# A two-layer hybrid trunk on 8 cores: interleaved spatial-gating stage, prefetches in flight together, the first eight weight blocks cast on chip, and weight copies stored in other passes

## What is computed

```
h = x
xn = rmsnorm(h);  p = xn @ ab_w_in                      # layer 0: pooling mixer A and short convolution B
h = h + concat(a_out, b_out) @ ab_w_out
h = h + square(relu(rmsnorm(h) @ mlp_w1[0])) @ mlp_w2[0]
xn = rmsnorm(h);  p = xn @ cd_w_in                      # layer 1
u, v = split(gelu(p[..., :1024]))
s = einsum('gts,bnsgc->bntgc', tril(w_s), layernorm(v)) + b_s     # 128-position chunks
c_out = u * s
d_out = stick_breaking_attention(q, k, v)               # 8 heads of 64, strictly causal
h = h + concat(c_out, d_out) @ cd_w_out
h = h + square(relu(rmsnorm(h) @ mlp_w1[1])) @ mlp_w2[1]
return rmsnorm(h)
```

## Time and profile before

| | us |
|---|---|
| median of 3 runs | 2937.12 (2935.02 to 2939.16) |
| the profiled execution's own time | 2936.28 |
| its span on the slowest core, first to last instruction | 2934.7 |
| spans of the 8 cores | 2916.7 to 2934.7 |
| PE busy (matmuls) | 2804.6, 96% of the span |
| DVE, ACT, POOL busy | 1462.7, 1415.3, 1184.9 |

### The profile page before, as it was taken

One profiled execution on the slowest core, in us unless ns is written; L12 is line 12 of the kernel. 1 busy time (PEld: TensorE's weight loads), 2 busy tenths in 40 slices (PEclk: granted clock), 3 DMA queues, 4 the chain that ended last, 5 costly groups with the idle time before them and its releaser, 6 DMA issues.

```text
span 2934.7 us, 43323 instructions; the slowest of 8 cores (2916.7 to 2934.7 us)
## 1 busy us (share of the span) xinstructions
PE 2804.6 (96%) x13273; PEld 1198.4 (41%) x13273; DVE 1462.7 (50%) x1759; ACT 1415.3 (48%) x2407; POOL 1184.9 (40%) x1685
## 2 busy tenths in 40 slices
PE   8899989999999999899999999999999989999998
PEld 3344433444444343344444344444444434444443
DVE  3501245544636555875655464453565675645003
ACT  3343353646447464355545354544655455544342
POOL 4211135344333554635543534443365535641110
PEclk9999999999999999999999999999999999999999
DMA  7878892455767999746786235565375586756222
GB/s 162 169 164 185 181 239 79 114 120 139 191 200 136 192 181 150 187 102 141 147 165 199 64 96 124 112 155 180 83 133 121 109 213 128 137 105 173 87 79 86
DMA packets 456912, 420.17 MB, mean 143 GB/s; under 512 B 310256, under 2 KB 334960, under 8 KB 456688
## 3 DMA queue, kind: packets, MB, share of 16 engines
q1 hardware_dynamic: 387424, 228.46, 34.4%
q0 software_dynamic: 69264, 188.95, 29.8%
HBM read 304.20 MB, written 89.13 MB: 134 GB/s over the span
## 4 chain that ended last, share of the span: by engine, by line
PE 81%; DMA 7%; DVE 3%; ACT 3%; issue 3%; POOL 2%; SPq 0%; DVEq 0%; ACTq 0%; POOLq 0%
PE ps L555 76%; PE ps L1240 3%; PE ps L1309 2%; DMA ring<-wblk 2%; DMA Wk<-Wq 1%; DMA stg<-xT 1%; DMA h<-hsp 1%; DVE P L1251 1%; DMA h<-xT 1%; POOL ps_76 L964 1%; ACT ps L545 0%; DVE h L732 0%; POOL ps_79 L964 0%; SPq L548 0%; DMA oT<-stg 0%
## 5 line engine op out<-in xcount | busy, mean ns | idle before, releaser
L555 PE MATMUL ps<-X_45,ring 128*128 128x512 bf16 x4864 | 1091.7, 380 | 1.4 <-ACT mix L545 1.3
L545 ACT ACTIVATE ps<-ps 128x512 f32<-128x512 f32 (+3 forms) x832 | 574.6, 699 | 566.6 <-PE ps L1240 313.6
L1265 POOL TENSOR_TENSOR Wq<-P 128x1022 bf16<-128x1022 f32 (+2 forms) x320 | 530.9, 1659 | 511.1 <-DVE P L1251 475.8
L555 PEld LDWEIGHTS ps<-X_45,ring 128*128 128x128 bf16 x4864 | 460.8, 98 | 571.0 <-issue 41.5
L555 PE MATMUL ps<-mix,ring 128*128 128x512 bf16 x2816 | 660.4, 381 | 3.3 <-DVE h L732 2.4
L732 DVE TENSOR_TENSOR h<-ps,h 128x512 f32<-128x512 f32 x384 | 265.0, 691 | 747.3 <-PE ps L555 735.4
L1251 DVE TENSOR_TENSOR_SCAN P<-ps,carry,cbs 128x512 f32<-128x512 f32 x384 | 487.5, 1278 | 229.8 <-ACT ps L545 197.3
L591 POOL DMA_DIRECT2D ring<-wbf x540 | 296.9, 552 | 645.2 <-PE ps L555 517.9
L555 PE MATMUL ps<-ffB,ring 128*128 128x512 bf16 x2048 | 483.8, 379 | 0.0
L555 PEld LDWEIGHTS ps<-mix,ring 128*128 128x128 bf16 x2816 | 264.8, 98 | 339.2 <-issue 42.6
L555 PE MATMUL ps<-X_44,ring 128*128 128x512 bf16 x1280 | 297.6, 388 | 25.4 <-DVE h L732 9.2
(11 more groups left out here) (115 smaller groups left out, 1402.5 us busy)
## 6 DMA issues: line engine op xcount, KB each, us to landing
ring<-wbf POOLq DMA_DIRECT2D x540, 256.0 KB, 4.4
ring<-wblk POOLq DMA_DIRECT2D x180, 256.0 KB, 7.0
wbf<-ring SPq DMA_DIRECT2D x180, 256.0 KB, 6.1
stg<-xT SPq DMA_DIRECT2D x96, 256.0 KB, 4.6
h<-xT SPq DMA_DIRECT2D x64, 256.0 KB, 10.1
hsp<-h SPq DMA_DIRECT2D x64, 256.0 KB, 5.9
h<-hsp SPq DMA_DIRECT2D x64, 256.0 KB, 9.1
oT<-mixf SPq DMA_DIRECT2D x32, 256.0 KB, 7.3
```

Of the source, the lines that this page charges most:

```text
L545: return Req("act", lambda e: e.activation(out=out, in_=in_, func=func, **kw), reads, writes, dur, bias=bias)
L555: ins = pe.matmul(out, lhsT=l, rhs=r, start=(first and i == 0), stop=(last and i == n - 1), skip_group_check=True)
L1265: yield Req("pool", lambda e: e.tensor_tensor(out=W3[:, :, 0:w - 1], in0=P[:, :, 1:w], in1=P[:, :, 0:w - 1], op=ALU.subtract), [LP], [LWq] ...
```

## The change

Seven edits, in the words of the code:

1. Start (`start_x`, `first_block`, `ring_fiber`, `alloc`): the first 8 weight blocks are loaded as float32 into staging buffers (`wst`, laid over kT and Wk, which are not yet in use) by DMAs on SP and on ACT, and cast into ring slots 0 to 7 by a copy on ScalarE (odd n) or GpSimd (even n). Half of the first eight x loads are issued on ACT. The loads of the second x tile wait for nothing, and the ring's own loads begin with block 8.
2. Weight copies (`ring_fiber`, `nokeep` in `build`): the first 16 loads of all are not stored in F00 but at their second use, in F01. Of the 72 loads of S00 every odd-numbered one is not stored either: its block is read as float32 once more, and stored, in S01.
3. `prefetch_x`: loads, squares and scales are fibers of their own, so that up to three `stg` loads are out at once.
4. `stage_M`: u and v groups alternate; in the second tile each pair is followed by a k head, behind a wait for the earlier attention's end that moves up with it.
5. `chain_v`: the four copies out of PSUM on ScalarE become one product on VectorE, with the scale broadcast along 128 columns; the estimates of the value matmuls and the bias are a little longer.
6. `to_out`: the store of an even channel block is a fiber of its own, held back by some 4 us of scheduled PE time where the next stage is another tail pass; the odd stores of the last tile are issued on ACT; `finbusy`, for which the next MLP waits, ends with the last of 8 stores.
7. The load of the constants `cb` is no longer held behind the first ring loads.

```diff
@@ alloc
+        w0, _ = sb("wst0", [128, 4, 1024], F32, self.off)
...
+        w1, _ = sb("wst1", [128, 4, 1024], F32, self.off)
+        self.wst = [w0, w1]
...
-        self.slots = Pool(range(RING))
+        self.slots = Pool(range(8, RING))
@@ ring_fiber
+        yield lambda: self.nload >= 8
         for n, b in enumerate(self.order):
+            if n < 8:
+                continue
             slot = yield self.slots
-            gate = []
-            if n < 8:
-                gate = [self.Lh[3][0]] if n < 4 else [self.Lh[3][1]]
-                yield lambda: gate[0].w is not None
...
-            if b not in self.Lwbf:
+            if b not in self.Lwbf and n >= 16 and not (n % 2 and self.nokeep[0] <= n < self.nokeep[1]):
                 self.Lwbf[b] = LT("wbf")
                 self.busy.add(slot)
                 self.M.spawn(self.keep_block(slot, b), 0.5)
             self.loaded[n] = slot
...
+    def first_block(self, n):
+        slot = n
+        yield lambda: self.Lwst[n].w is not None
+        src = self.wst[n // 4][:, n % 4]
+        if n % 2:
+            yield self.act(self.ring[:, slot, :], src, AF.Copy, [self.Lwst[n]], [self.Lring[slot]], 1024, False)
+        else:
+            yield Req("pool", lambda e: e.tensor_copy(out=self.ring[:, slot, :], in_=src), [self.Lwst[n]],
+                      [self.Lring[slot]], 1.7)
+        self.loaded[n] = slot
+        self.nload += 1
@@ to_out
+            if c % 2:
+                yield from store(c, buf, L, key)
+                self.p_stg.free(b)
+            else:
+                self.M.spawn(store(c, buf, L, key), 0.0)
+
+        def store(c, buf, L, key):
+            if c % 2 == 0 and then_tail:
+                t0 = L[0].w.fin + 4.0
+                yield lambda: self.S.free["pe"] > t0
+            r = self.dma(self.oT[s, c * 128:(c + 1) * 128, gs].rearrange("p (a n) -> p a n", a=2), buf, L, [], key)
+            if c % 2 and self.hnext is None and t == 1:
+                r.eng = "act"
+            o = yield r
...
@@ prefetch_x
-            for c in range(8):
+            def one(c, b, t=t, ev=ev):
+                yield from self.square(0, c, t, self.stg[:, b, :], self.Lstg[b], ev)
+                self.p_stg.free(b)
+
+            def load(c, gs=gs):
                 b = yield self.p_stg
                 yield self.dma(self.stg[:, b, :], self.xT[s, c * 128:(c + 1) * 128, gs], [], [self.Lstg[b]], ("stg", b))
-                yield from self.square(0, c, t, self.stg[:, b, :], self.Lstg[b], ev)
-                self.p_stg.free(b)
+                return b
+            for c in range(8):
+                b = yield from load(c)
+                self.M.spawn(one(c, b), 0.3)
...
+            def dst(c, m, Lm, g, t=t, load=load, scale=scale, left=left):
+                b = yield from load(c)
+                self.M.spawn(scale(c, b, m, Lm, g), 0.3)
@@ start_x
         for c in range(8):
-            yield self.load_h(self.xT, None, 0, 0, 0, c)
+            r = self.load_h(self.xT, None, 0, 0, 0, c)
+            r.eng = "sp" if c % 2 == 0 else "act"
+            yield r
+        for n in range(4):
+            yield wload(n, "sp" if n % 2 == 0 else "act")
+        for n in range(8):
+            self.M.spawn(self.first_block(n), -0.4)
...
-            r.reads = r.reads + [self.Lh[5][0]]
...
@@ chain_v
-            yield Req("pe", fn, [Lvn, self.Lwmt], [self.Lbank[b2]], 0.25, bias=-1.0, slack=0.6)
-            for g in range(4):
-                gs = slice(g * 128, (g + 1) * 128)
-                yield Req("act", (lambda g, gs: lambda e: e.activation(
-                    out=vt[:, gs], in_=self.bank(b2)[:, gs], func=AF.Copy, scale=cf[:, 64 + g:65 + g]))(g, gs),
-                    [self.Lcf], [self.Lbank[b2], Lvt], 0.27)
+            yield Req("pe", fn, [Lvn, self.Lwmt], [self.Lbank[b2]], 0.25, bias=-1.0, slack=0.8, wslack=0.2)
+            yield Req("dve", lambda e: e.tensor_tensor(
+                out=vt[:].rearrange("p (g t) -> p g t", g=4), in0=self.bank(b2).rearrange("p (g t) -> p g t", g=4),
+                in1=cf[:, 64:68].unsqueeze(2).to_broadcast([128, 4, 128]), op=ALU.mult),
+                [self.Lcf], [self.Lbank[b2], Lvt], 0.72, bias=-0.5)
@@ stage_M
             for g in range(4):
+                yield from gate_u(g, t, g == 0)
+                yield from gate_v(4 * t + g)
                 if t == 1:
+                    if g == 0:
+                        yield from self.need_attention(2 * s + u)
+                    yield from head(g, self.kT, self.LkT, u * UT)
+        for x in sl[0:4]:
+            self.release(x)
...
@@ build
+        n = sum({"F": 88, "M": 20}[x[0]] for x in self.stages[:4])
+        self.nokeep = (n, n + 72)
```

More of the change, by code:

```diff
@@ new lines, in gate_v, with head @@
+        def gate_v(n):
+            v = yield self.p_v
+            self.vbusy += 1
+            yield from self.group(movpairs(sl, n), [self.Lring[x] for x in sl[0:4]] + [LX[k][n // 4] for k in range(8)],
+                                  self.chain_v(s, u, n, v))
+        def head(a, dst, Ldst, d0):
+            sl = yield from self.take(1)
+            for t in range(2):
+                ts = slice(t * TT, (t + 1) * TT)
+                ev = copy_evac(dst[:, a, d0 + t * TT:d0 + (t + 1) * TT], [Ldst[a][d0 // TT + t]], "act")
+                yield from self.group(self.wpairs(sl[0], X, ts), [self.Lring[sl[0]]] + [LX[k][t] for k in range(8)], ev)
+            self.release(sl[0])
@@ L1177, in stage_M @@
-        yield from heads(self.kT, self.LkT, u * UT)
         sl = yield from self.take(4)
@@ L1184, in stage_M @@
             self.release(x)
-        yield from heads(self.qT, self.LqT, 0)
+        for a in range(4):
+            yield from head(a, self.qT, self.LqT, 0)
         self.M.spawn(self.attention(s, u), 0.4)
```

87 lines of the change are left out of this document (42 added, 45 removed).

## The result

The changed kernel takes 2923.33 us (median of 4 runs, 2920.36 to 2927.80); the kernel before, on the same chip, 2938.14 (2935.02 to 2945.05). The ratio is 0.9948, interval 0.9925 to 0.9970: some 15 us faster. The forecast was 41 us, and its range ended at 2922, 1 us short. In some runs one die, or both, runs at a lower granted clock and the time is longer, so wholes are compared over the undisturbed runs alone and given as a ratio to the kernel before, timed on the same chip, with a 95% interval, and nothing is read from e10_prefetch (all six runs disturbed) and e17_changed (five of six).

A forecast was written before the change was run, and what follows sets the result against it. The kernel was taken as PE-bound, with 130 us of idle PE in 2934.7 us, lost where stages meet. The terms summed to -41 us against 2936.3, giving 2895 us, with a range of 2873 to 2922.

The forecast's parts named there:

- the start: First 140 us: earlier loads of x and blocks and fewer stores cut waits and clock loss, -8 us (-14 to +3).
- F10: Stage F10: x loads in twos and threes spare some waits, -4 us (0 to -10).
- the tails: Starts of S10 and S11: even stores behind some loads of h leave PE fewer waits, -6 us (-14 to +3).
- the M stages: Four M stages: spread value steps and the product on VectorE cut idle time, -17 us (-23 to +4).
- The rival of the waiting start: Start: same bytes on the same 16 engines, so the waits stay; term 0, 2903 us; chance 0.15.
- M00's entry: Entry of M00: x loads in twos and threes end ScalarE's wait that delays PE, -5 us (0 to -7).
- the +3: Four M stages: the fourth V block gets its slot only after the third k head, +3 us (0 to +12).
- S00: -8 forecast: First tail pass: 36 stores moved out lower the DMA share, so transposes land sooner, -8 us (0 to -16).
- The forecast's line: Transposes: landing time linear in DMA share, 6.9 us at 1.04 and 3.6 at 0.57, giving 5.4 at 0.83.
- S01 and F01: Stages taking the moved stores: +3 us in S01, +1 in F01 (0 to +16).
- the slower case, the SP queue in S01: S01: stores waiting on SP delay transposes behind them; with 20 such waits 2953 us; chance 0.05.
- the rival of the stores that only change place: S00 keeps late transposes (0, not -8) and S01 pays 16, not 4; 2915 us; chance 0.18.

The follow-up runs named there:

- e10_prefetch: The kernel before with only the change's prefetch of x; all six runs were disturbed, so nothing is read from it.
- e17_changed: By its name the changed kernel timed again, not described further; five of six runs were disturbed, so nothing is read from it.
- e9_M: The kernel before with only the M edit (new group order and the product on VectorE); ratio 0.9976 to the kernel before.
- e12_stores: The kernel before with only the moved weight-copy stores; ratio 0.9977 to the kernel before.
- e2_keepall: The changed kernel with every weight copy of the first tail pass stored in that pass again; ratio 0.9977 to the kernel before.
- e16_prefetch2: The kernel before with only the change's prefetch of x, run once more; ratio 1.0002 to the kernel before.
- e4_oldout: The changed kernel with the final norm's output stores as before the change; ratio 0.9909 to the kernel before.
- the gate: The changed kernel with second x tile and float32 blocks waiting for the first tile's sixth piece, blocks loaded from SP alone; ratio 0.9926 to the kernel before.

## Why the prediction was wrong

Of the 26 us that are missing, 13 are the start, 6 F10, 4 the tails, 3 the M stages with their entry, and 5 lie between the median core and the slowest; S01, F01 and F11 came out 5 better than forecast.

**The start: -8 forecast, +5 measured** (start and F00). This is 13 of the 26 us that are missing. The step that failed is "with a DMA share of 0.79 there is room to be quicker". 0.79 is the mean over 140 us. The windows of the kernel before, then of the changed one:

```profile
10.00:20.00 10.00, 10.00 (x48) 4.49 (x47) 1.63 (x3) 5.19 (x9) 2.82 (x5) 1.00 0.93 169
20.00:30.00 10.00, 8.14 (x37) 3.36 (x35) 3.76 (x6) 2.63 (x6) 2.14 (x4) 1.00 1.03 227
```
```profile
10.00:20.00 10.00, 6.00 (x14) 1.61 (x15) 0.32 (x1) 5.89 (x11) 0.99 (x1) 0.64 1.00 332
20.00:30.00 10.00, 10.00 (x41) 4.30 (x40) 6.00 (x8) 2.81 (x5) 1.45 (x2) 0.85 0.95 304
```

The engines were nearly full before, too, where x lands. The old gates held blocks and second tile back until x was in; the change took the gates away, twice the bytes move per us, and the last square of the first tile ends at 17.34 us in place of 13.57. The rival of the waiting start (term 0, 2903) was nearer, and still too kind: it left out that the neighbours can make x later. The rule of the Trainium skill behind it ("DMA: Bandwidth & Descriptors", section "Issuing engines are not separate DMA queues") says that DMAs of several issuers interleave on the same 16 engines. The trace agrees, with a share of 1.00 from 10 to 20 us. The second queue as such did no harm: with it taken away the last square ended at 20.4 in place of 17.4 (medians of the cores), and the start was 28.6.

The two waits that the term was priced by stayed. The one for the second tile, 5.84 us in the earlier trace rows, of which half was to go, is 7.13, and the longest for VectorE's addition is 2.4 as before. The wait for the second tile was not one for landed bytes alone: in both kernels VectorE scales its eight blocks while PE waits. The scaling before, then PE's wait, the last squares and the scaling now:

```profile
36.80 5.39 DVE L674 SCALAR_TENSOR_TENSOR X_44<-h,cfs,ms 128x512 bf16<-128x512 f32 x8 [0.67 <-ACT ms L664]
```
```profile
44.96 11.41 PE L559 MATMUL ps<-X_44,ring 128*128 128x512 bf16 x40 [7.13 <-DVE X_44 L690]
31.51 2.69 ACT L549 ACTIVATE X_44<-h 128x512 bf16<-128x512 f32 x5
39.44 5.38 DVE L690 SCALAR_TENSOR_TENSOR X_44<-h,cfs,ms 128x512 bf16<-128x512 f32 x8
```

The last squares of the second tile no longer wait for a load, and PE waits longer all the same.

**M00's entry: -5 forecast.** Over the last 25 us of F00 and the first 15 of M00, PE's waits for VectorE's sums of squares shrank, from 3.8 to 1.9 us on the mean of the cores, but a new wait took their place: the first group is now a u group, and its block is late.

```profile
368.34 0.58 PE L559 MATMUL ps<-X_45,ring 128*128 128x512 bf16 x1 [4.54 <-DMA ring<-wblk]
```

Such waits went from 0.2 to 2.4 us on the mean of the cores, so that the two together are 4.3 us after 4.0. No term of the prediction has it: the +3 was for the attention's V blocks behind the k heads, where none of the six cores waits for a block.

**The M stages: -17 and +3, with the entry -19; measured -16.5.** Right in these stages, and by the edit that was named (e9_M: -15.0), though a part of that is a wait that moved into F00 (see e9_M). The product on VectorE takes 686 to 692 ns (691 was taken), and the copies on ScalarE are gone. Wrong is the bound on what is left, under 3 us idle in each window: two of the four have 4.3 and 3.7. Each stage still loses 2.2 us where a value step waits for VectorE's product of the one before.

```profile
385.07 0.38 PE L1150 MATMUL ps<-wmt,vn_85 128*128 128x128 bf16 x4 [0.94 <-DVE vt_82 L1154]
...
394.74 0.38 PE L1150 MATMUL ps<-wmt,vn_83 128*128 128x128 bf16 x4 [1.27 <-DVE vt_88 L1154]
```

**S00: -8 forecast, -7.9 measured, by the way that was argued, with one step of another size.** On the mean of the cores PE waits 4.5 us for transposes in place of 10.7, and the clock takes 2.6 in place of 6.0. The slowest core alone would say that the DMA share did not fall (1.03 in its window of S00). Over all cores it did fall. From 915 to 1155 us, which lies in S00 on every core, the mean share is 1.09 at 172 GB/s before, and 0.97 at 143 now; the median transposition lands in 7.0 us before and 5.9 now (means of the eight cores, which range from 5.8 to 9.7 and from 5.2 to 6.7); on six cores the share fell, on cores 2 and 3 it is 1.04 both times. Core 1 before and now, its window and its transposes:

```profile
915.00:1155.00 240.00, 230.72 (x1108) 94.90 (x1106) 140.87 (x138) 132.91 (x230) 124.68 (x152) 0.99 1.09 173
Wk<-Wq SPq DMA_TRANSPOSE x48, 6.9
```
```profile
915.00:1155.00 240.00, 238.21 (x1155) 98.42 (x1154) 141.40 (x141) 132.05 (x227) 128.16 (x157) 1.00 0.96 144
Wk<-Wq SPq DMA_TRANSPOSE x50, 5.6
```

With the stores moved alone (e12_stores) the means are 0.99, 142 GB/s and 6.0 us; with all stores put back into the changed kernel (e2_keepall) 1.08, 172 and 6.7. So moving the stores does this, with the other edits or without them. Mis-sized is the step from bytes to share: the bytes per us fell by 29 GB/s, near the forecast's 34 (9.4 MB in 280 us), but the share by 0.12 and not 0.21. The forecast's line also took its landing time from 940:1160, where core 1 had a share of 1.14, and its share, 1.04, from 900:1180. That the sum came out at -7.9 all the same is in part luck: with the stores alone S00 is 6.5 shorter by the median and 2.5 by the mean, and PE's waits hardly fall.

**S01 and F01: +4 forecast; S01 0, F01 +1.** S01's share is 0.77 (0.85 forecast), and its transposes land in 4.6 us (5.6). PE waits for none of them on any of the six cores. With that the slower case, the SP queue in S01, falls, and the rival of the stores that only change place with it. SP's waits for ring loads did grow, to 401.3 us in 138 from the 356.9 of the earlier trace rows, but no transposition in S01 reached PE late.

**F10: -4 forecast, +2.4 measured.** VectorE's waits for `stg`, from which the term was argued (76.9 us in 17 over the whole span), did go:

```profile
DVE X_44 L804 <- DMA stg<-xT: 5.7, 4, 3.2
```

But PE's idle time in the first 125 us of F10 is 15.0 us on the mean of the cores after 14.1: what held PE there was not these loads. It waited 3.7 us for VectorE's product into mix, and now waits 3.4 for a GpSimd subtraction and 2.2 for a GpSimd step of the pooling (means of the cores). The prefetch alone has F10 1.5 longer (e16_prefetch2), and with the old outputs it is 1.3 shorter (e4_oldout), but the thirteen profiles with the new prefetch lie between 367.8 and 370.5, so what makes the 2.4 stays open.

**The tails: -6 forecast, S10 +0.4 and S11 -2.3.** The step that failed is that even stores behind the loads of h leave PE fewer waits. Idle time did fall, from 10.0 to 9.1 us in S10; but waits of 6.6 for squares of h, on the slowest core most of it in one piece, stand where several short ones stood, and the clock loss went from 0.6 to 3.4 us (means of the cores).

**The slowest core.** Terms were summed on one core, and the metric is the slowest of eight. The terms as measured sum to -18, with F11, for which nothing was forecast, to -20; the median core gained 21 and the slowest 16. The late transposition goes with how the cores part: on core 5, the quickest, it took 5.77 us and S10 292.4; on core 3 10.88 and 308.3.

Of "what would show it", two signs named as wrong are there: idle PE is 118 us, over 100, and VectorE is the releaser in M. The lower end of the range, 2873, speaks of four large terms and adds three.

## What to carry to other kernels

A wait that holds a transfer back may be what lets the urgent one through: before it is taken away, read the DMA share of the few microseconds in which the urgent bytes land (0.93 here), not that of the whole stretch (0.79), and let the rest wait for them. A queue that issues both loads and transpositions makes a load as late as the transposition ahead of it (10.88 us here). One long stall can cost more than the same time in short ones: in S10, at idle times of 9.1 to 11.9 us with the new outputs and 8.8 to 10.5 with the old, the clock took 3.4 to 4.8 and 0 to 2.0. Read a share on every core before a step is called failed or right: the slowest core of S00 showed no fall, the mean of eight did. Price edits that meet in one queue together, and run each alone: here one edit kept 15 us in its own stages, of which the whole saw 7, and two gave nothing alone.

## What was not expected of the hardware

The issue of one transposition on SP took 5.8 to 12.1 us at the head of S10 on the eight cores, at a DMA share of 0.90, and 1.2 us in its shortest rows. The granted clock of the start was 0.64 in 10 to 20 us, with the lower level of 1.2 GHz from 12.7 to 22.9, after PE had stood for 2.79 us and while it stood for 1.54, 1.24 and 0.75 ahead of norm matmuls; it was 1.00 up to 30 us with the gate. One program's cores differ by 30 us in one execution: between cores 3 and 5 16 of it in S10, 8 in S11, 7 in F00 and 6 in F10, and 8 the other way in S00.
